# Grouped heads' attention steps between the differential heads', early head transposes, and small loads moved

## The reference, cut to what matters

```python
h = rms_norm(x, pre_mix_norm[l]);  proj = h @ w_in[l]          # 2464 columns
a_out = neighbourhood_attention(na_q, na_k, na_v, na_rel_bias[l])
b_out = diff_attention(...)   # softmax(s1) - lam * softmax(s2), then an rms norm over each head
c_out = gqa_attention(axial_rope(norm(gq_q)), axial_rope(norm(gq_k)), gq_v)   # 4 heads on 2 k/v heads
d_out = mla_attention(...)    # latents normed and projected up by mla_w_uq, mla_w_ukv; rope
x = x + rms_norm(concat(a_out, b_out, c_out, d_out) @ w_o[l], post_mix_norm[l])
x = x + rms_norm(ffn(...), post_ffn_norm[l])
```

## Time and profile before

| | us |
|---|---|
| median of 3 runs | 2028.98 (2027.85 to 2031.43) |
| the profiled execution, its own time | 2027.56 |
| its span, first to last instruction | 2025.8 |
| PE busy, share of the span | 1875.1, 93% |
| DVE busy | 1136.7, 56% |
| ACT busy | 922.2, 46% |
| POOL busy | 179.9, 9% |

### The profile page before, as it was taken

How to read it: one execution, slowest core, us unless ns; L and a number is a source line. 1 busy time by engine, 2 the same in 40 slices (tenths; PEclk the granted TensorE clock), 3 DMA queues, 4 the chain that set the end, 5 groups by cost and what they waited for, 6 DMA issues and landing times. The chain is left out here.

```text
span 2025.8 us, 28967 instructions
## 1 busy us (share of the span) xinstructions
PE 1875.1 (93%) x11496; PEld 1634.8 (81%) x11496; DVE 1136.7 (56%) x1647; ACT 922.2 (46%) x1267; POOL 179.9 (9%) x213
## 2 busy tenths in 40 slices
PE   4888999898899989899999999999969999989998
PEld 4657999775799978779998879998648998768997
DVE  3665555676655568664445455445655445765443
ACT  3364444445544446555344454435234344564432
POOL 0400000040000001001000000101420010100000
PEclk8989999898999999799999999999979999999999
DMA  5602555550255555324554534454715554435451
GB/s 180 236 5 94 167 186 186 178 183 30 74 186 186 186 176 161 125 84 167 186 187 168 179 109 166 168 206 152 215 49 171 186 187 167 167 109 177 172 206 63
DMA packets 185356, 313.07 MB, mean 155 GB/s; under 512 B 18878, under 2 KB 67572, under 8 KB 185268
## 3 DMA queue, kind: packets, MB, share of 16 engines
q1 hardware_dynamic: 182595, 304.24, 44.1%
q0 software_dynamic: 1376, 4.38, 0.8%
q10 hardware_dynamic: 1296, 3.24, 0.5%
HBM read 309.90 MB, written 1.94 MB: 154 GB/s over the span
## 5 line engine op out<-in xcount | busy, mean ns | idle before, releaser
L1404 DVE TENSOR_TENSOR w_lo<-raw,w_hi 128x2048 fp32r<-128x2048 f32 (+2 forms) x290 | 651.5, 2278 | 307.2 <-ACT w_hi L953 306.4
L953 ACT ACTIVATE w_hi<-raw 128x2048 fp32r<-128x2048 f32 (+2 forms) x290 | 533.3, 1876 | 110.1 <-PE tr L1938 63.8
L1936 PE MATMUL acc<-w_hi,aux_hi 128*128 128x512 f32 x688 | 269.6, 392 | 12.4 <-DVE aux_lo L1896 12.4
L1937 PE MATMUL acc<-w_lo,aux_hi 128*128 128x512 f32 x688 | 268.8, 391 | 0.0
L1938 PE MATMUL acc<-w_hi,aux_lo 128*128 128x512 f32 x688 | 268.2, 390 | 0.0
L1936 PE MATMUL up<-hT_hi,w_hi 128*128 128x256 f32 x864 | 246.3, 285 | 8.1 <-ACT proj L1335 5.1
L1936 PE MATMUL acc<-w_hi,hT_hi 128*128 128x512 f32 (+2 forms) x608 | 238.9, 393 | 8.9 <-DVE w_lo L1404 8.0
L1938 PE MATMUL up<-hT_hi,w_lo 128*128 128x256 f32 x864 | 245.4, 284 | 0.0
L1937 PE MATMUL up<-hT_lo,w_hi 128*128 128x256 f32 x864 | 245.4, 284 | 0.0
L1936 PE MATMUL tr<-hT_hi,w_hi 128*128 128x256 f32 x864 | 244.9, 283 | 0.0
L1937 PE MATMUL tr<-hT_lo,w_hi 128*128 128x256 f32 x864 | 244.5, 283 | 0.0
(11 more groups left out here) (344 smaller groups left out, 2460.4 us busy)
## 6 DMA issues: line engine op xcount, KB each, us to landing
raw<-in_mlp_w_up SPq DMA_DIRECT2D x64, 1024.0 KB, 6.6
raw<-in_mlp_w_down SPq DMA_DIRECT2D x64, 1024.0 KB, 5.4
raw<-in_ffn_w_gate_up SPq DMA_DIRECT2D x88, 512.0 KB, 4.7
raw<-in_ffn_w_down SPq DMA_DIRECT2D x22, 1024.0 KB, 4.9
raw<-in_w_in SPq DMA_DIRECT2D x16, 1024.0 KB, 7.4
raw<-in_sb_w_in SPq DMA_DIRECT2D x12, 1024.0 KB, 6.0
raw<-in_moba_w_in SPq DMA_DIRECT2D x12, 1024.0 KB, 5.5
raw<-in_nsa_w_in SPq DMA_DIRECT2D x10, 1024.0 KB, 5.2
```

The source lines that it names most:

```text
L953: nc.scalar.activation(w_hi[:, p0.slot, 0:p0.floats], raw[:, p0.slot, 0:p0.floats], ACT.Copy)\
L1404: nc.vector.tensor_tensor(w_lo[:, p0.slot, 0:m], raw[:, p0.slot, 0:m], f32(w_hi[:, p0.slot, 0:m]), ALU.subtract).then_inc(sem["lo_ready"], 1)
L1936: nc.tensor.matmul(dst, hi, whi, start=first, stop=False)
L1937: nc.tensor.matmul(dst, hi, wlo, start=False, stop=False)
```

## The change

- **Step order.** The grouped heads' steps 12 to 15 go between the differential ones: `STEP_ORDER`. Constants such as `GQ_FIRST` now are positions in that order. `diff_norm` moves to index 18, `diff_gain` to 20, the second `pair_out_lo` stays at 21. The wait of the first latent v product for `od_ready` (the end of `diff_gain`) becomes one for `od_taken` (the copy at the head of `diff_norm`).
- **Early jobs.** Eight of the ten jobs (neighbourhood, grouped, latent) are done inside the last chunk of the projection, between its two pieces (`jobs_early`). The two differential jobs come at index 1 of the steps.
- **Small loads.** SP issues pieces 4 to 9 in their order, with `first` behind piece 4, the later vectors behind piece 5, layer 0's seven row loads behind piece 7 and the bias behind piece 9. Layer 1's seven row loads go to just before layer 1's bias. The later vectors are turned in `A_1`, not in `A_0`.
- **Convolution weights.** Two more buffers for `lag_weight`, in tables that are no longer in use there, so all six tables are made at the start of `conv_stacks`.

```diff
-DF_FIRST, GQ_FIRST, ML_FIRST = 4, 12, 16
+STEP_ORDER = (0, 1, 2, 3, 4, 5, 12, 6, 7, 13, 8, 9, 14, 10, 11, 15, 16, 17, 18, 19)
+NA_LAST, DF_LAST, GQ_LAST = (max(STEP_ORDER.index(i) for i in range(a, b)) for a, b in ((0, 4), (4, 12), (12, 16)))
+GQ_FIRST, ML_FIRST = (min(STEP_ORDER.index(i) for i in range(a, a + 4)) for a in (12, 16))
+JOBS_EARLY, JOBS_A = 8, 10
...
+            def load_layer_rows(l):
+                for dst, src in rows[ROWS_PER_LAYER * l:ROWS_PER_LAYER * (l + 1)]:
+                    sp.dma_start(dst, src).then_inc(sem["row_landed"], 16)
+            beside = {SLOTS: load_first, SLOTS + 1: load_later_vectors, SLOTS + 3: lambda: load_layer_rows(0),
+                      SLOTS + 5: lambda: load_bias(sp, 0)}
+            for at in range(SLOTS + 6):
                 load([plan.pieces[at]])
...
+                if at in beside:
+                    beside[at]()
...
                     if ph.variant == "A" and ph.row == 1 and LAYERS[1:2] == [("A", 1)]:
+                        load_layer_rows(1)
                         sp.wait_ge(sem["x_written"], 4)
                         load_bias(sp, 1)
...
-                for k in range(EARLY):
+                for k in range(CONV_PE):
                     lag_weight(k)
...
                     stack_in(k)
-                    lag_weight(k)
...
+                    if ph.mix is not None and ph.mix.kind == "mixA" and i == 4:      # ACT, ahead of chunk 4's copy
+                        for j in range(JOBS_EARLY):
+                            _, dst, scale = jobs_for("A")[j]
+                            evac_job(j, dst, scale, n["pt_ready"])
...
+                        if ph.mix is not None and ph.mix.kind == "mixA" and (i, k0) == (4, 0):      # PE
+                            jobs_early()
...
+            def jobs_early():
+                pe.wait_ge(sem["na_ready"], n["na_ready"] + NA_H)
+                for j in range(JOBS_EARLY):
+                    if j == 2:
+                        pe.wait_ge(sem["gq_prep"], n["gq_prep"] + 1)
+                    if j == 4:
+                        pe.wait_ge(sem["ml_prep"], n["ml_prep"] + 1)
+                        pe.wait_ge(sem["kcat_a"], n["kcat_a"] + 2)
+                    job(j, jobs_for("A")[j][0], n["pt_evac"])
...
-            def A_0(ph):
+            def A_1(ph):
                 if ph.l == 0:
                     turn_vectors((1, 2, 3), "vec_later_landed", 16 * 6)
...
+                    if i == 1:
+                        diff_jobs()
...
                         if j == ML_FIRST:
-                            pe.wait_ge(sem["od_ready"], n["od_ready"] + 1)
+                            pe.wait_ge(sem["od_taken"], n["od_taken"] + 1)
...
-                    if i == 15:
+                    if i == DF_LAST + 4:
                         diff_norm()
-                    if i == 17:
+                    if i == DF_LAST + 6:
                         diff_gain()
```

More of the change, by code:

```diff
@@ L232, in make_plan @@
                       "na_flip": 1, "na_ready": NA_H, "aux_tr": 2, "aux_hi": 3, "aux_lo": 3,
-                      "lam_ready": 1, "lam_exp": 1, "hT_tr": 1, "kcat_a": 2, "od_ready": 1})
+                      "lam_ready": 1, "lam_exp": 1, "hT_tr": 1, "kcat_a": 2, "od_ready": 1, "od_taken": 1})
             phases.append(Phase("mixA", l=l, uq=uq, ukv=ukv, counts=c))
@@ L544, in pair @@
                     steps.append(dict(qt=qt, heads=heads, bias=bias and [b[:, S * qt:S * qt + S] for b in bias],
[L545 removed]
+                                      scale=scale, diff=diff, apart=True))
             def head(q, k, v_col, row, k_tile):
@@ L564, in pair_steps @@
                            A_IN + 128 * (2 * t + u) + 64, HD * u, 6 + t) for u in range(2)])
-            return steps
+            for i in range(GQ_STEPS.start, GQ_STEPS.stop):
+                steps[i]["apart"] = False
+            return [steps[i] for i in STEP_ORDER]
         def pair_bank(i, u):
@@ L696, in jobs_for @@
                         (two(2048 + 192, 96, 96), tiles[0:96, 13:15, :], -96.0 ** -0.5),
-                        (ks[0], tiles[0:96, 15:17, :], 1.0), (ks[1], tiles[0:96, 17:19, :], 1.0)]
+                        (ks[0], tiles[0:96, 15:17, :], 1.0), (ks[1], tiles[0:96, 17:19, :], 1.0),
+                        (two(col("df_q")), tiles[:, 4:6, :], 1.0), (two(col("df_k")), tiles[:, 6:8, :], 1.0)]
             qs = [(two(2 * P * j), tiles[:, 2 * j:2 * j + 2, :], 1.0) for j in range(4)]
@@ L746, in _ @@
                 (100, "mla_kv_norm"))], "vec_landed")
-            for at in range(SLOTS):
-                load([plan.pieces[at]])
[L750 to L762, removed]
@@ L763, in _, with load_later_vectors @@
-            load_bias(sp, 0)
-            at = SLOTS + 1
+            def load_later_vectors():
+                load_rows([(0, vec_rows[1], "conv_dw_b_2"), (8, vec_rows[1], "conv_ln_g_2"),
+                           (16, vec_rows[1], "conv_ln_b_2")], "vec_later_landed")
+                pos = A["nsa_cmp_pos_2"][0].rearrange("j l d -> (j l) d")
+                sp.dma_start(vec_rows[1][24:88, :], pos).then_inc(sem["vec_later_landed"], 16)
+                taps = A["conv_dw_w_2"][0].rearrange("j (k c) -> (j k) c", c=P)
+                for half in range(2):
+                    rows_here = VEC_ROWS[2 + half]
+                    sp.dma_start(vec_rows[2 + half][0:rows_here, :], taps[P * half:P * half + rows_here, :])\
+                      .then_inc(sem["vec_later_landed"], 16)
@@ new lines, in load_first @@
+            def load_first():
+                sp.dma_start(region[:, 2048:2048 + n_first], A["first"]).then_inc(sem["row_landed"], 16)
+            def load_layer_rows(l):
[3 more added lines that the diff above has]
+                      SLOTS + 5: lambda: load_bias(sp, 0)}
@@ L1181, in mix_A, with diff_turned @@
                 nc.scalar.activation(lam[:, 0:2], lam[:, 2:4], ACT.Exp).then_inc(sem["lam_exp"], 1)
-                for j, (_, dst, scale) in enumerate(jobs_for("A")):
-                    if j == 2:
+                def diff_turned():
+                    for j in range(JOBS_EARLY, JOBS_A):
+                        _, dst, scale = jobs_for("A")[j]
+                        if j > JOBS_EARLY:
+                            evac_job(j, dst, scale, n["pt_ready"])
+                            continue
                         act.wait_ge(sem["pt_ready"], n["pt_ready"] + j + 1)
```

84 lines of the change are left out of this document (43 added, 41 removed).

## The result

The change makes the kernel faster, by a good half of what was forecast: 2003.16 us median of 4 runs (2001.41 to 2005.04) against 2028.41 for the kernel before beside it, a ratio of 0.9877 with a 95% interval of 0.9858 to 0.9896. That is 25 us; 45 were forecast, and the time lies above the forecast's range of 1975 to 1996. The profiled execution took 2001.45 us with a span of 1999.6. Lines of the kernel after stand some 15 to 50 further down: L1971 to L1973 are the three products of a weight block, L2058 the jobs, L2234 the scores, L2247 the transposes of the probabilities, L2369 the convolution.

What follows compares the result with a forecast made beforehand. PE, busy 93% of the span, was taken to wait mainly for a small transfer (15.9 us) and POOL (13.2 us), with differential steps DVE bound. Gains less losses summed to 45.4 us: 1983.6 us by the median, range 1975 to 1996.

Steps and rivals of the forecast that it cites:

- Two more at 2.0 to 4.1 us fit into the 10.46 us in which POOL waited to send rows: Convolution: two more tables fit into POOL's waiting time without delaying tile 0; part of a 14.0 us gain.
- rival F: Projection: POOL's rotations, stretched beside DVE, hold up PE; slower than before, 2038 us at a factor of 2.2; chance 0.02.
- The mean's last four of 16 products follow: Convolution's end: only four products, 0.9 us, remain after DVE's taps, so the mean ends at 1477.9, not 1491.88.
- Layer 1's rows: Seven row loads ahead of layer 1's bias lengthen PE's wait: 4.5 us lost, between 3.0 and 8.3.
- rival C: Late load or POOL in layer 0, or layer 1's rows at their upper bound: 4 to 9 us less gain; chance 0.13.
- Start of layer 0: PE's wait for the taps goes and chunk 3 starts at 53.9, not 73.52: gain 19.6 us, taken as 20.
- Tails: End of each attention: norm at 18 again holds the last steps' divisions; gain 0.3 us, bounds -2 and +1.5.
- Head of the attention: Chunk 4's end to fifth scores takes 8.1 us in layer 0: gains 6.9 and 7.4 us in the two layers.
- Rival D: Clock falls over the early jobs, so the piece behind takes up to 11.3 us, not 5.65; 1989 to 1995; chance 0.05.
- Step order: Attention: mixed grouped and differential steps balance DVE and PE at 5.2 us a cycle; gain 5.8 us a layer.
- Rival B: Clock falls in the attention of one or both layers, costing 5 us each; 1988.6 to 1993.6 us; chance 0.2.
- the forecast's own signs of being wrong: Pieces 10 and 11 late, clock 0.5 in either attention, or row loads holding SP for other than 3 to 8 us.

Runs made afterwards that it cites:

- The two experiments on either side: Changed kernel with tables of tiles 4 and 5 made after the rows are sent out (1999.38 us), or behind their stacks as before the change (2011.94 us, one execution).
- a_conv_late: Changed kernel with the tables of tiles 4 and 5 made by POOL after the rows are sent out: 1999.38 us median, ratio 0.9861 to the kernel before.
- a_all: Changed kernel with layer 1's rows before the feed-forward loop, two tables behind the rows sent out, norm spread over three places, lambda's exponentials early: 1981.50 us, ratio 0.9764.

## Why the forecast was wrong

The direction was right, and each stall that was to go did go. The gain was forecast 19 us too high, in six places.

*Convolution, 7.1 us: the step "Two more at 2.0 to 4.1 us fit into the 10.46 us in which POOL waited to send rows" failed.* They fit into POOL's own time, and the rows went out on the same beat. But DVE was not free: the last table ends at 1409.90, and DVE's pair of splits, begun at 1408.43, takes 5.82 us for 4.48. The overlap is 1.47 us, and the first split is 1.34 longer. The split frees a slot, so SP's two pieces start 1.3 us later and push against the rows sent out, which land 3.1 us later; through POOL's queue this reaches tiles 0 and 4, and the stack of tile 4 comes 5.5 us after the time assumed. The two experiments on either side show that the place of the tables is the cause; the links between it and the late landing are read from the profiles, and none was changed by itself. The Trainium skill has the rule that was missed (SBUF — State Buffer, SBUF: two separate sides): a VectorE operation with two inputs in SBUF and a GpSimd operation that reads SBUF contend for a shared pair of ports, which is an exclusive lock, and whichever comes second is blocked until the first ends. Here the trace agrees, and also the earlier trace rows: the table of 14.44 us ends 1.8 us after DVE's last tap, as if it had waited for the whole row of taps. The forecast had used it only to price rival F.

The 7.1 us are not all this step's. Tile 4 began at 1453.36, or 1472.6 on the time axis of before, 5.2 us after the 1467.4 forecast. The other 1.9 are a second slip, "The mean's last four of 16 products follow": all 16 stand behind tile 5. With the 9.5 us that the forecast gives to tiles 4 and 5 the mean would end at 1480.6 and the gain be 11.3, below its bound of 12; to come near 14.0 both tiles must run at full clock. In `a_conv_late` they had it (7.0 us); in the changed kernel they took 8.7.

*Layer 1's rows, 3.4 us.* The term was seen with its place and mis-sized: 7.9 us for 4.5, near the upper bound of 8.3 (rival C). In the six other profiles with the rows in this place it is 8.5 to 9.3, over the bound. What it left out is that packets stay queued when SP has issued them. The issue cost 4.8, about as taken; the bias behind the rows' packets then took 3.6 us more to issue. The row move alone on the kernel before costs 8.4.

*Start of layer 0, 2.7 us.* Chunk 1 ended at 35.1 (forecast 35.0) and the latents were turned from 37.3 (36.9). Then, just behind PE's hole of 1.9 us, the clock fell (0.5 from 37.7 on), and chunk 2 took 12.5 us for 11.3. In five of the other profiles it did not, and chunk 3 starts at 54.2 to 54.3 where 53.9 was forecast. The taps and pieces 10 and 11 were in time.

*Tails, 3.0 us.* `diff_norm` at 18 was taken to hold the last steps' divisions as before, for a gain of 0.3 with bounds of -2 and +1.5; it cost 0.6 and 1.8. The bounds held. The step to doubt was "again": at 15 the norm lies among steps that have others behind them, at 18 it stands before the last minimum, with nothing behind for PE.

*Head of the attention, 2.7 us.* It took 8.7 and 10.1 us for the 8.1 priced (8.2 in layer 1): the clock (0.81, 0.83; at 1.00 layer 0's head takes 7.4), and in layer 1 the table load of 1.28 us, whose cover, the ten jobs, the change took away. The early jobs themselves cost 5.1 for 5.3. Rival D did not happen.

*Step order, 2.3 us.* Rightly reasoned, for the order does balance DVE and PE and the clock was 1.00, but a cycle of three took 5.4 to 6.2 us (PE's scores at 99.36, 104.74, 110.92 and 116.64) for 5.2. The estimate of PE's work was right: over these three cycles PE is busy for 4.95, 5.41 and 5.37 us, 5.2 on average. What failed is that a cycle would take no longer than that; each also has 0.35 to 0.8 us in which PE is idle, which the forecast had only as its lower case ("if each cycle lost another 0.5 us, 4.3"). Rival B, the clock, is real in eight of eighteen layers at 3.3 us each, in place of the 5 given; the fall begins in the head, not in the differential steps that the forecast watched.

Against these stand about 2 us in the other direction, most of it chunk 3 of layer 0, which ran at full clock all through.

The range failed because its low end took each mechanism at its price and its high end one mishap at a time. The convolution had bounds of 12 and 14.3, built on POOL's order alone, and no rival for it. But that step alone does not put the time outside: with it mended (`a_conv_late`) the median is 1999.38, still above 1996. Of the forecast's own signs of being wrong one was there: the clock was at 0.5 in both attentions for a few microseconds, in heads and tails. The other two were not; the rows held SP for 4.8 us, inside the 3 to 8 allowed, and cost 7.9 all the same.

## What to carry to other kernels

An idle stretch of one engine is a cover only if what shares its ports, and the loads that wait for that, are idle too: ask of work moved into a hole what it does to the instruction beside it. A load moved out of one stall's queue lands in another queue; look for one with slots to spare (here the feed-forward loop), and count what its packets take, not only what its issues do. When work is taken from the head of a stage, ask what it was covering (here a table load and a short scalar chain).

## What the runs showed of the hardware

- Repeated rows are slow transfers: seven loads, 288 KB in 1408 packets (by their sizes, 256 bytes each and 128 for lambda's), landed 8.8 to 10.9 us after their issue began. For 3.5 us of this the queue moved only 20 to 27 GB/s, where the weights moved at over 400; and SP took 3.6 us more for the bias behind them, though it had issued them in 4.8.
- The same 23 us of steps ran at a granted clock of 1.00 or 0.84 from one execution to the next, after a head in which PE had holes of 2 us. Filling such a hole can give more than its length: the spread norm took out waits of 3.1 us and left the clock in both tails at 1.00, and again in `a_all`.
- A table that POOL makes in 1.99 us takes 4.04 when one of DVE's splits has begun before it, and took 13.02, 13.90 and 14.44 us while DVE ran its taps, ending 1.8 us after the last tap each time. DVE's taps were not slowed (23.8 us in all kernels). In the other order, POOL first and 1.47 us of overlap, DVE's split took 3.62 us for 2.28.
